# A Conformer, SSD and MoE step: first layer in another order, second pointwise product in rounded and rest halves

## What is computed

```
sh, sc, g = silu(cond) @ ada_w[i] + ada_b[i]          # 6 rows of 1024, for each stream
# layer 0
u = h @ pw1_w + pw1_b          # h = x * (1 + sc) + sh, 1024 -> 2048
u = u[:, :1024] * sigmoid(u[:, 1024:])
v = depthwise_conv(u, 31 taps) + dw_b
v = silu(layer_norm(v))
f = v @ pw2_w + pw2_b          # 1024 -> 1024
x = layer_norm(ALPHA * x + g * f)
# after each mixer
out[e] = (silu(x_e @ w_gate[e]) * (x_e @ w_up[e])) @ w_down[e] * gate_e     # 16 experts, 3 x 1024 x 1024
x = layer_norm(ALPHA * x + g * scatter_add(out))
```

## Time and profile before

| | us |
|---|---|
| median of 3 runs (2453.04 to 2470.23) | 2455.43 |
| the profiled execution | 2459.2 |
| its span, first to last instruction | 2457.2 |

### The profile page before, as it was taken

The page is one execution under the profiler, slowest core; times in us unless marked ns, Lnnn a source line. Parts: engine busy times, 40 slices in busy tenths (PEclk is TensorE's granted clock), DMA queues, the critical chain, the costliest instruction groups (busy, mean ns, idle before and its releaser), DMA issues. The chain is left out here.

```text
span 2457.2 us, 24510 instructions
## 1 busy us (share of the span) xinstructions
PE 2180.2 (89%) x9570; PEld 1351.6 (55%) x9570; DVE 1755.5 (71%) x1889; ACT 1148.3 (47%) x1399; POOL 356.6 (15%) x203
## 2 busy tenths in 40 slices
PE   6998778699999999949899999999759999999992
PEld 3544433466666666635656557466536666666661
DVE  1898733799899889825374653654968898899893
ACT  2112222566666666632512333234236666666672
POOL 1000004111110111040011101101320111110113
PEclk8988889899999999969899999999979999999996
DMA  7145703599999999930023124124249999999992
GB/s 313 73 168 242 340 0 107 194 367 372 362 367 380 356 368 368 359 126 26 26 86 65 35 81 95 52 80 109 78 146 350 359 371 371 362 375 369 372 372 92
DMA packets 51666, 561.18 MB, mean 228 GB/s; under 512 B 6240, under 2 KB 6256, under 8 KB 20448
## 3 DMA queue, kind: packets, MB, share of 16 engines
q1 hardware_dynamic: 37584, 508.80, 53.7%
q0 software_dynamic: 13968, 50.82, 8.1%
HBM read 523.42 MB, written 36.18 MB: 228 GB/s over the span
## 5 line engine op out<-in xcount | busy, mean ns | idle before, releaser
L1472 DVE TENSOR_TENSOR w_l<-ring,w_h 128x2048 fp32r<-128x2048 f32 x384 | 869.8, 2286 | 68.5 <-ACT w_h L1028 66.3
L1028 ACT ACTIVATE w_h<-ring 128x2048 fp32r<-128x2048 f32 x384 | 731.9, 1916 | 324.4 <-PE bank L554 162.9
L552 PE MATMUL bank<-w_h,xin_h 128*80 128x512 f32 x1024 | 407.7, 398 | 3.2 <-DVE xin_l L1492 1.9
L553 PE MATMUL bank<-w_l,xin_h 128*80 128x512 f32 x1024 | 403.1, 394 | 0.0
L554 PE MATMUL bank<-w_h,xin_l 128*80 128x512 f32 x1024 | 400.2, 391 | 0.0
L1267 POOL DMA_INDIRECT z_rows<-hT,slot_i x32 | 101.6, 3174 | 982.0 <-DVE hT L1503 982.0
L552 PE MATMUL bank<-w_h,hidT_h 128*80 128x512 f32 x512 | 206.5, 403 | 36.2 <-DVE hidT_l L1486 36.2
L552 PEld LDWEIGHTS bank<-w_h,xin_h 128*80 128x80 f32 x1024 | 151.9, 148 | 93.9 <-DVE xin_l L1492 11.3
L554 PE MATMUL bank<-w_h,hidT_l 128*80 128x512 f32 x512 | 202.3, 395 | 0.0
L553 PE MATMUL bank<-w_l,hidT_h 128*80 128x512 f32 x512 | 201.7, 394 | 0.0
L554 PEld LDWEIGHTS bank<-w_h,xin_l 128*80 128x80 f32 x1024 | 152.0, 148 | 85.9 <-issue 0.9
(11 more groups left out here) (249 smaller groups left out, 2876.5 us busy)
## 6 DMA issues: line engine op xcount, KB each, us to landing
ring<-w_stream SPq DMA_DIRECT2D x234, 2048.0 KB, 9.9
z_rows<-X POOLq DMA_DIRECT2D x15, 512.0 KB, 8.8
X<-z_rows SPq DMA_DIRECT2D x15, 512.0 KB, 5.3
h_rows<-scr POOLq DMA_DIRECT2D x10, 512.0 KB, 3.9
ln_gb<-ln_rows POOLq DMA_DIRECT2D x4, 1024.0 KB, 6.8
ring<-w_stream SPq DMA_DIRECT2D x4, 1024.0 KB, 5.1
X<-x_in SPq DMA_DIRECT2D x1, 2560.0 KB, 25.8
y_out<-X SPq DMA_DIRECT2D x5, 512.0 KB, 2.6
```

Of the source, the lines that this page charges most:

```text
L552: pe.matmul(out[0:SLOTS, :], ah[:, c, :], wh[:, k, :], start=(first and k == 0), stop=False)
L553: pe.matmul(out[0:SLOTS, :], ah[:, c, :], wl[:, k, :], start=False, stop=False)
L1028: A(w_h[m % NB][:, :, :], src, ACT.Copy).then_inc(s["high_ready"], 1)
L1472: V.tensor_tensor(w_l[m % NB][:, :, :], src, w_h[m % NB][:, :, :].bitcast(F32), ALU.subtract)\
```

## The change

Three things change.

1. The first layer is written in another order. The units of the first pointwise product are 1 MB each, one for each chunk, and stand between the modulation units (`FIRST`). x is loaded in two halves, and the first chunk's product starts, feature block by feature block, as soon as half of shift and scale is there. Modulation units are multiplied in pairs before each of the chunks 3 to 7; the mean's first four parts go ahead of the last four modulation units. `CONV_DVE` has two groups of one chunk and three of two.
2. The second pointwise product is made of three fp32r matmuls, with the rounded half and the rest of the weights (`pw2_high` on ACT, `pw2_low` on DVE, in halves of a unit) and of v (`v_high`, `v_rest`). The first two token tiles follow v feature block by feature block. The bias row is loaded into all partitions, DVE multiplies it with the gates, and one instruction for each tile puts ALPHA * X and that product into X ahead of the residual, which is then a plain sum.
3. The experts' units are loaded in two halves of 1 MB, each with a semaphore of its own (`half_landed`); each half is requested when the same half of the unit three back has passed `low`, and `high` waits for its own half.

```diff
-CONV_DVE = ((0,), (1, 2), (3, 4), (5, 6, 7))
+CONV_DVE = ((0,), (1,), (2, 3), (4, 5), (6, 7))
...
+ADA_COLS = ((0, 2, 1, 3) + tuple(range(4, 12)), tuple(range(12)))
+FIRST = (["a"] * 4 + ["p"] * 3 + ["a", "a", "p"] * 5 + ["a"] * 10)
...
-            sp.dma_start(X[:, :, :], x_in).then_inc(s["x_loaded"], 16)
+                if j == 1:
+                    sp.dma_start(X[:, :, 0:512], x_in[:, :, 0:512]).then_inc(x_half[0], 16)
...
             def load(u):
                 j = u % R
-                free(u - R)
-                w = UNIT // 2 if U_SSD <= u < U_MOE1 and SSD_UNITS[u - U_SSD][0] == "bc" else UNIT
+                if in_moe(u):
+                    for h in range(2):
+                        free(u - R, (h,))
+                        w = slice(h * HALF, (h + 1) * HALF)
+                        sp.dma_start(ring[j][:, w], w_stream[u, :, w]).then_inc(half_landed[j][h], 16)
+                    return
+                free(u - R, (0, 1))
...
-            build_hT(0)
-            hT_whole(0)
-            for c in range(4):
+            for k in range(4):
+                first_turn(k)
+            for u in (2, 3):
+                ada_mm(0, u)
+                ada_tr(0, u)
+            pe.wait_ge(s["mT_ready"], 8)
+            for k in range(4):
+                first_chunk(k)
+            first_turn(4)
+            first_turn(5)
+            for k in range(4, 6):
+                first_chunk(k)
+                first_turn(k + 2)
+            first_chunk(6)
+            first_chunk(7)
+            pw1(1)
+            pw1(2)
+            ada_done = 4
+            for c in range(3, KC):
+                ada_pair(ada_done)
+                ada_done += 2
                 pw1(c)
...
+            def pw2_part(i, k, w_h, w_l):
+
+                t = i % NT
+                vh, vl = v_h[:, k, t * P:(t + 1) * P], v_l[:, k, t * P:(t + 1) * P]
+                pe.matmul(bank[i % 8][:, :], vh, w_h[:, k, :], start=(k == 0), stop=False)
+                pe.matmul(bank[i % 8][:, :], vl, w_h[:, k, :], start=False, stop=False)
+                ins = pe.matmul(bank[i % 8][:, :], vh, w_l[:, k, :], start=False, stop=(k == KC - 1))
+                if k == KC - 1:
+                    ins.then_inc(s["f_mm"], 1)
+
             for nb in range(2):
-                w = unit_wait(U_PW2, nb)
-                for t in range(NT):
+                low = ring_low[(U_PW2 + nb) % R][:, :].rearrange("p (k n) -> p k n", n=512)
+                for k in range(KC if nb == 0 else 0):
+                    pe.wait_ge(s["pw_low"], k // 4 + 1)
+                    pe.wait_ge(s["v_low"], k + 1)
+                    for t in range(2):
+                        pw2_part(t, k, pw_h[0], low)
+                pe.wait_ge(s["pw_low"], 2 * nb + 2)
+                for t in range(2 if nb == 0 else 0, NT):
...
             for k in range(KC):
                 act.wait_ge(s["centered"], k + 1)
                 if k >= 2:
                     act.wait_ge(s["var_mm"], k - 1)
                 A(sq[:, k % 2, :], v[:, k, :], ACT.Square).then_inc(s["sq_ready"], 1)
+            pw2_high(0)
+            gate_evac(0)
+            pw2_high(1)
             act.wait_ge(s["var_ready"], 2)
             A(rstd, rstd, ACT.Sqrt).then_inc(s["rstd_ready"], 1)
             for k in range(KC):
                 act.wait_ge(s["normed"], k + 1)
                 A(v[:, k, :], v[:, k, :], ACT.Silu, bias=cln_b[:, k:k + 1], scale=cln_g[:, k:k + 1])\
                     .then_inc(s["v_ready"], 1)
+                act.wait_ge(s["v_ready"], k + 1)
+                A(v_h[:, k, :], v[:, k, :], ACT.Copy).then_inc(s["v_high"], 1)
+            pw2_high(2)
+            pw2_high(3)
             normalise(0)

             def high(u0, E, m):
                 j = (u0 + 6 * (E % 16) + m // 2) % R
-                act.wait_ge(landed[j], 16 * ((u0 + 6 * (E % 16) + m // 2) // R + 1))
+                act.wait_ge(half_landed[j][m % 2], halves(u0 + 6 * (E % 16) + m // 2))
...
-            pool.dma_start(pwb[0:1, :], pw2_b).then_inc(s["pwb_loaded"], 16)
+            pool.dma_start(pwb, pw2_b[0:1].partition_broadcast(P)).then_inc(s["pwb_loaded"], 16)
...
-                ins = V.scalar_tensor_tensor(X[:, t, c], X[:, t, c], ALPHA, tmp[:, buf, :], ALU.mult, ALU.add)
+                V.tensor_tensor(X[:, t, c], X[:, t, c], tmp[:, buf, :], ALU.add).then_inc(out_sem, 1)
...
+            gb = [mrow.rearrange("p a b -> p (a b)"), pwb]
+            for c in range(2):
+                link(V.tensor_tensor(gb[c], pwb, gate_bc[:, c, :], ALU.mult))
+            for t in range(NT):
+                step(V.scalar_tensor_tensor(X[:, t, :], X[:, t, :], ALPHA, gb[int(t == NS)], ALU.mult, ALU.add))
+                if t in (1, 3):
+                    pw2_low(2 + t // 2)
```

More of the change, by code:

```diff
@@ L304, in shift_part, with in_moe, whole, halves @@
             return 0 if stage % 2 == 0 else 24
+        def in_moe(u):
+            return U_MOE0 <= u < U_SSD or u >= U_MOE1
+        def whole(u):
+            return 16 * len([i for i in range(u % R, u + 1, R) if not in_moe(i)])
+        def halves(u):
+            return 16 * len([i for i in range(u % R, u + 1, R) if in_moe(i)])
         def low_done(eng, E, m):
@@ L349, in used, with free @@
                 raise ValueError(u)
-            def free(u):
+            def free(u, hs):
                 for L, u0 in ((0, U_MOE0), (1, U_MOE1)):
@@ L370, in x_reload @@
                     sp.dma_start(X[:, t, :], z_rows[t * P:(t + 1) * P, :]).then_inc(x_back[t], 16)
-            for u in range(R, U_SSD + R):
+            for u in range(R, U_PW1[0] + 1):
+                load(u)
+            sp.dma_start(X[:, :, 512:D], x_in[:, :, 512:D]).then_inc(x_half[1], 16)
+            for u in range(U_PW1[0] + 1, U_SSD + R):
                 load(u)
@@ L398, in unit_wait @@
                 j = (u0 + k) % R
-                pe.wait_ge(landed[j], 16 * ((u0 + k) // R + 1))
+                pe.wait_ge(landed[j], whole(u0 + k))
                 return ring[j][:, :].rearrange("p (k n) -> p k n", n=512)
@@ L519, in _ @@
                 ins = pe.matmul(bank[2][:, 0:P], mean_w, v[:, k, SAMPLE:TOK], start=(i == 0), stop=(i == KC - 1))
-            ins.then_inc(s["mean_mm"], 1)
+                if i == KC - 1:
+                    ins.then_inc(s["mean_mm"], 1)
+            pe.wait_ge(s["glu_a"], 16)
+            for i in range(4):
+                mean_part(i)
+            ada_pair(20)
+            ada_pair(22)
+            for i in range(4, KC):
+                mean_part(i)
+            gates(0)
             for k in range(KC):
@@ L536, in _ @@
                     for k in range(KC):
-                        pe.matmul(bank[i % 8][:, :], v[:, k, t * P:(t + 1) * P], w[:, k, :], start=(k == 0), stop=False)
-                    ins = pe.matmul(bank[i % 8][:, :], ones[0:1, :], pwb[0:1, nb * 512:(nb + 1) * 512],
-                                    start=False, stop=True)
-                    ins.then_inc(s["f_mm"], 1)
+                        pw2_part(i, k, pw_h[nb], low)
             def product(E, m, out, ah, al):
@@ L658, in ssd_wait @@
                 u = ssd_unit(kind, g)
-                pe.wait_ge(landed[u % R], 16 * (u // R + 1))
+                pe.wait_ge(landed[u % R], whole(u))
                 return ring[u % R]
@@ L950, in hT_evac, with first_evac @@
                       scale=mT[:, L, sh + 8 + k, 0:1]).then_inc(s["hTs_ready"], 1)
+            def first_evac(k):
+                act.wait_ge(s["mT_ready"], 8 if k < 4 else 16)
+                act.wait_ge(s["hT_tr"], k + 1)
+                A(hT[:, k, 0:SAMPLE], bank[(3, 6)[k % 2]][:, :], ACT.Identity, bias=mT[:, 0, k, 0:1],
+                  scale=mT[:, 0, 8 + k, 0:1]).then_inc(s["hTs_ready"], 1)
             def gate_evac(b, b0=4):
@@ L1163, in wo_split @@
                 u = ssd_unit("out", g)
-                act.wait_ge(landed[u % R], 16 * (u // R + 1))
+                act.wait_ge(landed[u % R], whole(u))
                 if g:
@@ L1420, in _ @@
                                     1.0, None, ALU.add).then_inc(s["adab_ready"], 1)
-            hT_evac(0)
+            for k in range(KC):
+                first_evac(k)
             for chunks in CONV_DVE:
```

226 lines of the change are left out of this document (128 added, 98 removed).

## The result

The changed kernel takes 2378.01 us (median of 4 runs, 2376.49 to 2379.95) against 2454.23 for the kernel before; the ratio is 0.968, with a 95% interval of 0.9634 to 0.9726. The profiled execution of the changed kernel has a span of 2378.1, 79.1 less than the 2457.2 before. Here is where those 79.1 lie, by the same marks in both traces.

What follows compares the result with a forecast made beforehand. No single engine bounds throughout: DVE's convolution and mutual waits in the first layer, nearly full PE stopped by late weights in the experts. 2459.2 - 45 (first layer) - 30 (experts) = 2384, or 2380 on the median's basis; range 2355 to 2425.

Steps and rivals of the forecast that it cites:

- Start: First layer up to DVE's first product with the sigmoid: reordering saves loading time only, priced at 0, 4 either way.
- Convolution: First layer's convolution: new groups remove two waits (-11.7), one more chunk alone costs +3.7; net -8.
- To the last square: Convolution's end to last square, 27.1 before: less PE work left ahead of the mean, 13 to 18 after; -12.
- the 17.53: DVE's wait for the mean at the convolution's end, in us, put down to modulation units, gate rows and mean parts on PE.
- Second product: Last square to DVE's step behind the last tile, 99.6 before: fp32r matmuls and two tiles following v end at 72.4; -27.
- the 84.3: Time of the second pointwise product's matmuls before the change, within the 99.6 from last square to last product.
- Tail: End of the first layer: DVE's product, sum and statistics for each tile, slowed beside POOL; +2.
- Experts: Both expert stages: halves cure late weights, at most 33 to be had over 28 periods; -30 taken, trusting 428 GB/s.
- The floor of 34.73: Period for each expert without PE's 16.7 us of waiting for late hidden rows, against 35.92 before.
- Transfers bound in any case: Rival, experts: 369 GB/s is all this traffic gets, halves give nothing; 2410 (2400 to 2425), chance 0.22.
- start-up for each load: Rival, experts: each load pays its start-up, so twelve loads cost 5.0 more for each expert; 2550, slower, chance 0.06.
- The first layer gives less: Rival: later start, PE at the lower clock and a DVE-bound tail take 15 to 25 of the 45; 2395 to 2405, chance 0.09.

Runs made afterwards that it cites:

- run ten: Changed kernel with PE's order around the mean as before: all modulation units, then gate rows, then the eight mean parts; 2374.45 us.
- the fp32 run: Changed kernel with the second pointwise product in fp32 again, begun when all of v is there, bias and ALPHA * X still ahead in the stream; 2388.88 us.
- run one: Kernel before with only the experts' units loaded as two halves, each asked for and waited for by itself; 2427.33 us, ratio 0.9896.
- run six: Changed kernel with each half loaded as two loads of 0.5 MB, asked for and waited for together, 384 loads for a stage; 2373.28 us.

## Why the prediction was right, and where its steps were off

Forecast 2380, measured 2378; the sum of -75 against its own execution stands against -79.1.

**Start: 0 forecast, -2.5 measured.** Within the 4 either way. But the mark lay at 64.9 to 66.6 in the three traces with the old first layer and at 60.2 to 65.3 in the eleven with the new one, with medians of 66.5 and 61.1. So the new order probably shortens the start by some 4 or 5, where the prediction had it save loading time only; no run takes this apart.

**Convolution: -8 and -8.1.** Both waits went. The old groups in the new order cost 13.1, so the groups are worth more there than the prediction's 8: it had priced them against the old order of the modulation units.

**To the last square: -12 and -12.9, for another reason than the text had in front.** The prediction named three things on PE ahead of the mean: the last modulation units, the gate rows and the eight parts. Putting gate rows and parts back where they were costs nothing (run ten). By the traces the place is free because the last modulation unit has been loaded 30 earlier, with ten units and not sixteen behind the last chunk; no run tries this by itself. The row that I should have set beside the 17.53 was the one of 428 GB/s in the window just ahead of it, which I used only for the experts.

**Second product: -27 and -27.1, the size right and the parts wrong.** The prediction put it down to tiles of 24 short matmuls and to two tiles that follow v. By the runs, 12.4 are the row of ones and the bias, which the change moves to DVE and for which my text had no term of its own: it was inside the 84.3 that I subtracted. The other 14.7 are the three products and the following; without the following only 3.5 of them are left. Scaling 11.2 behind the last square (11.8 forecast) and the last tile 72.5 (72.4) fit, and that end was summed up from steps of its own, so the size isn't luck. The products with gates and the sums into X, hidden by forecast, are: with them in the stream the fp32 run has its last tile 86.7 behind, and the kernel before without bias, which hasn't them there, 87.2.

**Tail: +2 and +3.8, with another mechanism.** The sum into X took 2.82 beside POOL in one tile, but DVE was through with that tile just as the last one came. What was lost lies behind: DVE's last scaling of X took 2.46 beside POOL in place of 1.22, and the gather ahead of the first expert landed 9.0 after its issue, where it was 6.0. With early halves SP asks for the experts' next half 2.1 behind the gather, with whole units or late asking for the next load 4.3 behind it, in all fourteen traces and ahead of both stages. In the five runs that ask for whole units or ask late the gathers ahead of the two stages landed in 5.8 to 6.0, in the seven others, with early halves, in 9.3 to 10.3. The halves alone on the kernel before (run one) lengthen this stretch from 100.4 to 105.4. The prediction had no term for what the earlier requests collide with; that its +2 lies near the 3.8 is luck.

**Experts: -30 and -34.7.** The floor of 34.73 was right, and all of it was had; it comes to more than the 33 because a stage has 15 periods from its first to its last scatter, and the sum counted 14. That 369 GB/s weren't the limit is shown: the same bytes move faster with more, smaller loads, and with free halves ACT doesn't wait for the ring. Whether 428 GB/s can be had beside the gathers isn't shown, since at 382 PE already sets the pace. That lateness is the cause holds in part. Either of early request and early landing is enough, but half of the gain comes with two loads in place of one even without both, and for that the prediction had no term. The price for the added load, taken as 0.3 and hidden, isn't there at all: the earlier trace rows compared times from issue to landing, in which a load waits for the one ahead of it, and by that measure the loads of 0.5 MB in run six took 7.7.

**Rivals.** "Transfers bound in any case" and "start-up for each load" are both excluded by the periods with 96, 192 and 384 loads for a stage: 36.1, 34.70 and 34.70. "The first layer gives less" didn't come about: its stretches up to the first scatter gave 46.8 together, with 45 forecast. Its reading of the 17.53, as a wait for a PE that had just begun again, doesn't hold: PE idled 2.0 for its last modulation unit's load at 282, and then worked almost without a gap up to the mean.

What stays open: the time between the two experts' stages was 825 to 837 in executions of the same code for it. The changed kernel's profiled execution had 837.4, the highest, and its +2.5 is not a cost that these runs can give to the change.

## What to carry to other kernels

A transfer engine that is 99% busy need not be full: here 369 GB/s became 382 when its loads were split. Where another stretch of the same trace moves more, try splitting the loads, and let each piece be asked for or used by itself. The earlier request and the earlier use replaced each other here, so take the one that doesn't collide with other traffic (asking late and using early spared the gather 3 us). Before you credit faster arithmetic, give each small thing that goes with it a term of its own: a product with one row of weights cost PE more than one with 128, 1.24 for each tile against 0.86. And where an engine waits for a late step, look first at when that step's data were loaded, before moving instructions.

## What the runs showed of the hardware

Twice 1 MB, asked for at the same moment and used together, did better than 2 MB in one load: a period of 35.4 and not 36.1 (means of two stages, one trace each), with the times of asking and using the same. I had expected the added loads to cost something, and down to 0.5 MB they cost nothing that the period shows (34.70, at 382 GB/s).

DVE's operations on X of 128x1024 took 1.22 alone (at 417.01 in the kernel before) and 2.46 beside POOL, and its sum of 128x512 2.82 in place of 0.69, in the changed kernel as in the earlier trace rows.
